# Query spread and page mask as fp32r products of split factors, the own token's value products moved behind the loop, penalties in one VectorE operation

## What is computed

```python
gate = jnp.einsum('bshd,bnhd->bhsn', q, k_mean)         # 8 blocks of 256 past tokens
_, idx = lax.top_k(gate, ks)                            # keep 3 blocks per head
s_sel = jnp.where(ok_sel, s_sel - slopes * dist_sel, NEG)
p = jax.nn.softmax(concatenate([s_sel, s_own]), axis=-1)
o = einsum('bhqnj,bhqnjd->bqhd', p_sel, v_sel) + einsum('bhqj,bjhd->bqhd', p_own, v_own)
```

## Time and profile before

| what | value |
| --- | --- |
| median of the runs | 651.88 us (650.3 to 652.17) |
| the profiled execution | 652.33 us |
| its span, first to last instruction | 650.6 us |
| mean granted TensorE clock | 0.921 |
| TensorE busy | 580.1 us (89% of the span), 4100 products |
| VectorE busy | 406.6 us (62%), 608 instructions |
| ScalarE busy | 272.9 us (42%) |
| GpSimd busy | 133.9 us (21%) |

### The profile page before, as it was taken

How to read it: one execution, slowest core, us unless ns; L and a number is a source line. 1 busy time by engine, 2 the same in 40 slices (tenths; PEclk the granted TensorE clock), 3 DMA queues, 4 the chain that set the end, 5 groups by cost and what they waited for, 6 DMA issues and landing times.

```text
span 650.6 us, 10200 instructions
## 1 busy us (share of the span) xinstructions
PE 580.1 (89%) x4100; PEld 468.8 (72%) x4100; DVE 406.6 (62%) x608; ACT 272.9 (42%) x492; POOL 133.9 (21%) x205
## 2 busy tenths in 40 slices
PE   3869998899999899999988688779999999999997
PEld 2647776664554647566547587668999999999997
DVE  2423794589888799888664284446645566655541
ACT  1102213195857668563463152127333343433341
POOL 8110020075757476570000000000000000000000
PEclk9969999878979799797978798987999999999999
DMA  7997289437999989979850949625487746366600
GB/s 254 380 405 301 93 335 400 147 116 296 361 368 325 383 304 409 347 286 374 300 236 9 379 149 369 217 91 203 143 279 243 253 138 210 91 178 179 178 34 33
DMA packets 85198, 159.29 MB, mean 245 GB/s; under 512 B 2572, under 2 KB 61112, under 8 KB 81047
## 3 DMA queue, kind: packets, MB, share of 16 engines
q1 hardware_dynamic: 79328, 89.27, 41.3%
q0 software_dynamic: 5120, 67.71, 26.3%
q10 hardware_dynamic: 703, 1.67, 0.7%
HBM read 156.39 MB, written 2.72 MB: 245 GB/s over the span
## 4 chain that ended last, share of the span: by engine, by line
PE 68%; DVE 14%; DMA 8%; ACT 6%; issue 3%; ACTq 1%; SPq 1%; POOL 1%; DVEq 0%; POOLq 0%
PE acc L1211 15%; PE acc L1306 12%; PE acc L1307 12%; PE acc L1308 11%; PE chain L1330 5%; PE acc L1178 3%; DVE sall L862 2%; DVE prod L855 2%; DMA wring<-in_w_ada 2%; DMA wring<-in_w_out 2%; PE small L1368 2%; ACT L515 2%; DMA wring<-in_w_attn_proj 1%; DMA wring<-in_w_ffn_in 1%; PE chain L1332 1%
## 5 line engine op out<-in xcount | busy, mean ns | idle before, releaser
L1211 PE MATMUL acc<-hT,wring 128*128 128x264 f32 x576 | 160.4, 433 | 4.0 <-DVE hT L820 1.9
L933 DVE TENSOR_TENSOR wlo<-wring,whi 128x1024 fp32r<-128x1024 f32 (+2 forms) x92 | 101.9, 1108 | 99.0 <-ACT whi L515 98.3
L1211 PEld LDWEIGHTS acc<-hT,wring 128*128 128x128 f32 x576 | 118.6, 214 | 35.5 <-issue 10.8
L515 ACT ACTIVATE whi<-wring 128x1024 fp32r<-128x1024 f32 (+2 forms) x92 | 88.0, 963 | 118.6 <-PE acc L1308 94.0
L1306 PE MATMUL acc<-xlo,whi 128*128 128x264 f32 x416 | 123.9, 298 | 13.1 <-DVE xT L1081 7.0
L1307 PE MATMUL acc<-xhi,wlo 128*128 128x264 f32 x416 | 121.0, 291 | 0.0
L1308 PE MATMUL acc<-xhi,whi 128*128 128x264 f32 x416 | 120.9, 291 | 0.0
L487 POOL TENSOR_TENSOR cvT<-cvT,cprod 128x256 f32<-128x256 f32 x120 | 87.2, 727 | 81.7 <-ACT cprod L515 66.2
L1306 PEld LDWEIGHTS acc<-xlo,whi 128*128 128x128 f32 x416 | 81.3, 195 | 17.8 <-DVE wlo L933 8.2
L1307 PEld LDWEIGHTS acc<-xhi,wlo 128*128 128x128 f32 x416 | 81.7, 196 | 0.1
L1308 PEld LDWEIGHTS acc<-xhi,whi 128*128 128x128 f32 x416 | 81.2, 195 | 0.0
(11 more groups left out here) (222 smaller groups left out, 647.5 us busy)
## 6 DMA issues: line engine op xcount, KB each, us to landing
wring<-in_w_ada SPq DMA_DIRECT2D x24, 1024.0 KB, 8.1
wring<-in_w_ffn_in SPq DMA_DIRECT2D x22, 1024.0 KB, 6.6
wring<-in_w_in SPq DMA_DIRECT2D x12, 1024.0 KB, 18.1
wring<-in_w_ffn_out SPq DMA_DIRECT2D x16, 704.0 KB, 5.7
wring<-in_w_out SPq DMA_DIRECT2D x4, 1024.0 KB, 14.9
wring<-in_w_in SPq DMA_DIRECT2D x6, 512.0 KB, 9.6
wring<-in_w_in SPq DMA_DIRECT2D x4, 768.0 KB, 8.4
wring<-in_w_conv_proj SPq DMA_DIRECT2D x2, 1024.0 KB, 9.6
```

The source lines that it names most:

```text
L515: return nc.scalar.activation(out, in_, f, **kw)
L933: v.tensor_tensor(wlo[:, place, 0:n, :], w, whi[:, place, 0:n, :].bitcast(F32), ALU.subtract)\
L1211: ins = mm(bank[:, 0:R], w[:, k, P * t:P * t + P], src[:, k, :], start=k == 0, stop=k == KD - 1)
```

## The change

1. The bank `qs` gets the samples' queries twice, in rows 0 to 7 and 32 to 39. ScalarE copies both to `qsplit`, rounded to fp32r, and a third time to `snat`; VectorE subtracts the rounded rows from the bank in rows 32 to 39. `spread_query` is one fp32r product over 40 rows with `qsel`.
2. The distance penalty becomes a product of two rows (`posal`, fp32r) in place of the identity times a table; `inquad` and `pen` are fp32r too.
3. L988 and L990 become one operation with a table `bars` (the diagonal times NEG), made at the start.
4. The own token's probabilities are put aside for each sample (`powns`, in place of L1038); its product in `weigh_values` is gone. Behind the loop VectorE picks the diagonal, multiplies the own values (`vrow`), TensorE turns them (four products), and VectorE adds them to `oT`.
5. `snat`, `vrow`, `ptable` lie in other tensors; GpSimd makes the new tables at the start.

```diff
@@ -565,7 +584,10 @@
             bank = when_full(act, "qs")
-            freed(func(snat[:, :], bank[0:B, :], ACT.Copy), "qs")
+            act.wait_ge(consts, 3)
+            func(qsplit[32:32 + B, :], bank[32:32 + B, :], ACT.Copy).then_inc(qs_ready, 1)
+            func(qsplit[0:B, :], bank[0:B, :], ACT.Copy).then_inc(qs_ready, 1)
+            func(snat, bank[0:B, :], ACT.Copy).then_inc(qs_ready, 1)
...
+            bank = when_full(dve, "qs")
+            dve.wait_ge(qs_ready, 3)
+            freed(v.tensor_tensor(qsplit[32:32 + B, :], bank[32:32 + B, :], qsplit[32:32 + B, :].bitcast(F32),
+                                  ALU.subtract), "qs")
...
-                mm(qbc[b % 2][:, :], ident[0:B, b:b + 1].to_broadcast([B, P]), snat[:, :], start=True, stop=True)\
+                mm(qbc[b % 2][:, :], qsel[0:32 + B, b:b + 1].to_broadcast([32 + B, P]), qsplit[0:32 + B, :],
+                   start=True, stop=True)\
                     .then_inc(qbc_ready, 1)
...
-            to_rows("qs", qT, S, B)
+            bank = bank_for("qs")
+            for t in range(4):
+                nc.tensor.transpose(bank[0:B, P * t:P * t + P], qT[:, t, S:R], ident[:, :])
+                ins = mm(bank[32:32 + B, P * t:P * t + P], qT[:, t, S:R], ident[:, :], start=True, stop=True)
+            ins.then_inc(acc_full, 1)
@@ -985,10 +1012,8 @@
-                at_pen = mark(v.tensor_scalar(gate[:, :], gate[:, :], float(TOPK), NEG, ALU.is_ge, ALU.mult))
-                dve.wait_ge(dve_step, at_pen)
-                v.tensor_tensor(pen[:, :, :], gate[:, :].unsqueeze(2).to_broadcast([H, NB, H]),
-                                ident[0:H, 0:H].unsqueeze(1).to_broadcast([H, NB, H]), ALU.mult)\
+                v.scalar_tensor_tensor(pen[:, :, :], gate[:, :].unsqueeze(2).to_broadcast([H, NB, H]), float(TOPK),
+                                       bars[:, :].unsqueeze(1).to_broadcast([H, NB, H]), ALU.is_ge, ALU.mult)\
                     .then_inc(pen_ready, 1)
...
-                v.scalar_tensor_tensor(pown, s1[32:32 + B, PG, :], ident[32:32 + B, 32 + b:33 + b], rinv[32:32 + B, :],
-                                       ALU.mult, ALU.mult).then_inc(p_ready, 1)
+                v.tensor_tensor(powns[32:32 + B, b, :], s1[32:32 + B, PG, :], rinv[32:32 + B, :], ALU.mult)\
+                    .then_inc(own_ready, 1)
@@ -1322,14 +1363,12 @@
-                        ins = mm(pv[32 * q:32 * q + H, :], pg[:, g, :], vring[:, g, :], start=g < 4, stop=PG - 4 < g)
-                        if g == PG - 4:
-                            mm(pv[0:H, :], pown, vrow, start=False, stop=True)
+                        ins = mm(pv[32 * q:32 * q + H, :], pg[:, g, :], vring[:, g, :], start=g < 4, stop=PG - 4 <= g)
...
-                mm(mask_, ident[:, :], alib[:, :, :].rearrange("p g h -> p (g h)"), start=True, stop=False)
+                mm(mask_, posal[:, 0, :], posal[:, 1, :], start=True, stop=False)
                 for e in range(QU):
-                    ins = mm(mask_.rearrange("p (c j h) -> p c j h", c=CH, h=H), inquad[:, e, :],
+                    ins = mm(mask_.rearrange("p (c j h) -> p c j h", c=CH, h=H), inquad[0:H, e, :],
@@ -1049,7 +1074,18 @@
             for t in range(1, KD):
                 conv_branch(t)
+                if t == 1:
+                    dve.wait_ge(own_ready, B)
+                    step(v.tensor_tensor(powns[32:32 + B, :, :], powns[32:32 + B, :, :],
+                                         ident[32:32 + B, 32:32 + B].unsqueeze(2).to_broadcast([B, B, H]), ALU.mult))
+                    step(v.tensor_reduce(pown, powns[32:32 + B, :, :].rearrange("p b h -> p h b"), AX.X, ALU.add))
+                    v.tensor_tensor(vrow.rearrange("p (h d) -> p h d", d=DH), vrow.rearrange("p (h d) -> p h d", d=DH),
+                                    pown.unsqueeze(2).to_broadcast([B, H, DH]), ALU.mult).then_inc(ownrow_ready, 1)
                 if t == 2:
+                    dve.wait_ge(ownt_ready, 1)
+                    dve.wait_ge(o_ready, 2 * B)
+                    v.tensor_tensor(oT[:, :, S:R], oT[:, :, S:R], ownT.rearrange("p (t b) -> p t b", b=B), ALU.add)\
+                        .then_inc(ownt_ready, 1)
                     for k in range(AT):
...
-                    act.wait_ge(o_ready, 2 * B)
+                    act.wait_ge(ownt_ready, 2)
...
             turn_values(B - 1)
+            pe.wait_ge(ownrow_ready, 1)
+            for t in range(AT):
+                ins = mm(ownT[:, B * t:B * t + B], vrow[:, P * t:P * t + P], ident[32:32 + B, 32:32 + B], start=True, stop=True)
+            ins.then_inc(ownt_ready, 1)
             for t in range(2, KD):
```

More of the change, by code:

```diff
@@ L145, in program @@
         prT = sb("prT", [P, 384])
-        srows = sb("srows", [P, A])
-        snat, vrow = srows[0:B, :], srows[32:32 + B, :]
+        qsplit = sb("qsplit", [P, A], F32R)
+        qsel = sb("qsel", [P, B], F32R)
         ident = sb("ident", [P, P])
@@ L177, in program @@
         cmp1, cmp2 = (mrow[0:H, 0, 64 * e:64 * e + 64].rearrange("p (m n) -> p m n", m=NB) for e in range(2))
-        pen = sb("pen", [H, NB, H])
+        pen = sb("pen", [H, NB, H], F32R)
+        spots = pvm[:, P:2 * P]
+        powns = gs[:, :, 0:H]
         tiny = sb("tiny", [P, 64])
@@ L181, in program @@
                                        tiny[:, 32:40], tiny[32:32 + B, 40:48])
+        bars = tiny[0:H, 56:64]
         pmx, psum_, prin = tiny[:, 48:50], tiny[:, 50:52], tiny[:, 52:54]
         cvs = sb("cvs", [P, CT, B])
-        ptable = sb("ptable", [P, B * PG], I32)
+        ptable = pr[:, 256:384].bitcast(I32)
         lane = sb("lane", [P, 1])
@@ L241, in program @@
         spread_max, spread_sum = small[:, 0:H], small[:, 16:16 + H]
-        pv, pvT = chain, psT[:, 384:392]
+        pv, pvT, ownT = chain, psT[:, 384:392], small[:, 256:256 + AT * B]
         vec_in, x_in, c_in, st_in, pt_in = sem("vec_in"), sem("x_in"), sem("c_in"), sem("st_in"), sem("pt_in")
@@ L442, in _ @@
                 step(g.memset(slopes[:, h:h + 1], -2.0 ** (-8.0 * (h + 1) / H)))
-            step(g.iota(dists[:, :].rearrange("p (c j) -> p c j", c=CH), pattern=[[-PC * P, CH], [-1, PC]], base=PAST,
-                        channel_multiplier=-PC, allow_small_or_imprecise_dtypes=True))
-            step(g.tensor_tensor(alib[:, :, :], dists[:, :].unsqueeze(2).to_broadcast([P, PG, H]),
-                                 slopes[:, :].unsqueeze(1).to_broadcast([P, PG, H]), ALU.mult))
+            two = slice(0, 2)
+            step(g.iota(dists[two, :].rearrange("p (c j) -> p c j", c=CH), pattern=[[-PC * P, CH], [-1, PC]], base=PAST,
+                        channel_multiplier=0, allow_small_or_imprecise_dtypes=True))
+            step(g.affine_select(out=dists[two, :], in_=dists[two, :], compare_op=ALU.not_equal, fill=-float(PC),
+                                 base=-1, pattern=[[0, PG]], channel_multiplier=1))
+            step(g.iota(spots[two, :], pattern=[[1, P]], base=0, channel_multiplier=0,
+                        allow_small_or_imprecise_dtypes=True))
+            step(g.affine_select(out=spots[two, :], in_=spots[two, :], compare_op=ALU.not_equal, fill=1.0,
+                                 base=0, pattern=[[0, P]], channel_multiplier=1))
             step(g.memset(lower[:, :, :], 1.0))
@@ L449, in _ @@
                                  base=0, pattern=[[1, NB], [-1, NB]], channel_multiplier=0))
-            step(g.memset(inquad[:, :, :], 0.0))
+            step(g.memset(inquad[:, :, :].bitcast(F32), 0.0))
             for q in range(QU):
-                step(g.memset(inquad[:, q, 32 * q:32 * q + 32], 1.0))
+                step(g.memset(inquad[0:H, q, 32 * q:32 * q + 32].bitcast(F32), 1.0))
+            step(g.tensor_copy(posal[:, 0, :], spots[two, :]))
+            step(g.tensor_tensor(posal[:, 1, :].rearrange("p (g h) -> p g h", h=H),
+                                 dists[two, :].unsqueeze(2).to_broadcast([2, PG, H]),
+                                 slopes[two, :].unsqueeze(1).to_broadcast([2, PG, H]), ALU.mult))
+            step(g.memset(qsel[:, :].bitcast(F32), 0.0))
+            step(g.tensor_copy(qsel[0:B, :], ident[0:B, 0:B]))
+            step(g.tensor_copy(qsel[32:32 + B, :], ident[32:32 + B, 32:32 + B]))
+            step(g.memset(qsplit[:, :].bitcast(F32), 0.0))
             step(g.memset(headof[:, :], 0.0))
```

14 lines of the change are left out of this document (9 added, 5 removed).

## The result

| | before | changed |
| --- | --- | --- |
| median (range, runs) | 652.02 us (650.3 to 654.83, 4) | **634.68 us** (634.5 to 636.54, 4) |
| ratio, 95% interval | | **0.9736** [0.9698, 0.9775] |
| profiled execution | 652.33 us | 634.61 us |
| span, mean granted clock | 650.6 us, 0.921 | 632.9 us, 0.933 |

The change is faster by 17.3 us. The forecast was 7.6 us, and its range ended at 640. The order of the work came out as predicted, but the loop gained nearly twice as much.

The account below looks back on a forecast made before the run. The chain of waits was 68% TensorE, 14% VectorE. Gains of 10.4 us in the loop and penalties of 2.8 at start and end made -7.6: 644.7 us profiled, median 644.3; forecast 641.5 to 647, full range 640.0 to 651.5.

Parts of the forecast that it names:

- Ranking beside GpSimd: VectorE's block ranking, b=1 to 5, still ends with GpSimd's gather issue; only L990 goes, 1.0 us gained.
- GpSimd doesn't hold the ranking: Rival: the earlier arrival finds other gaps between GpSimd's additions; up to 3.7 us more gain, 640.6 us; chance 0.10.
- The mask: TensorE, mask to tile: five fp32r instructions replace ten; 1.0 to 1.1 us saved a cycle, 6.2 over six cycles.
- Narrow fp32r is no cheaper: Rival: each of the mask's five products costs as much as its pair; 2.0 us saved, not 6.2; 648.5 us; chance 0.27.
- The third part: TensorE's stretch of the cycle through mask, half a tile and turned maximum; from tile to next first sum forecast 0.
- The clock rival: Rival: TensorE idle or on tiny products before the mask lengthens lower-clock stretches; 12.9 us lost, 657.2 us; chance 0.09.
- The end: Behind the loop, last weighing to attention load: wait for the own row queues units 2 to 7; +2.1 us, bounds 0 to +4.
- The start: Before the loop: spread query adds matmuls, copies and a subtraction, first multiplication 1.4 later, 0.7 regained; +0.7 us.
- VectorE's idle time before the gate's copy gone: Sign that the forecast is right: VectorE, idle 0.74 us before the gate's copy, has no idle time there in b=1 to 5.
- L977's successor still at 0.60 beside additions: Sign that the forecast is right: this VectorE ranking operation still takes 0.5 us or more beside GpSimd's additions.
- b=6: Cycle where GpSimd adds nothing: VectorE's idle 0.74 and L990's 0.2 count in full; 0.95 us gained.
- cycle b=0: Loop's cycle where ScalarE is behind with four stores and the tap products: mask gain forecast as nothing.

Follow-up runs that it names:

- The fillers: The changed kernel plus three unread f32 products of 264 columns where TensorE waits for the penalty, each cycle: 629.05 us, ratio 0.9684.

## Why the prediction was wrong

**The failed step is "Ranking beside GpSimd".** It took one phase of the two engines for a rule: L977 ended 0.07 behind the additions and L988 with the issue, so the ranking would end with GpSimd's work whatever came earlier. What the rows fit is a smaller thing. A VectorE operation that reads two tensors in SBUF (L977) ends when the addition that is under way ends, not the last one. The additions follow one another every 0.85 (5.10/6). In the changed kernel the fifth ends at about 176.98 + 5 x 0.853 = 181.25, and L1004 is done there, at 181.27. The penalty's operation L1015 is held in its turn, by the sixth (0.39 us, where it has 0.21 in b=0 and 6). In the kernel before L977 happened to meet the sixth and last. In all cycles b=1 to 5 of both kernels the operation ends 0.07 to 0.08 us behind an addition. So an earlier gate moves the whole ranking, and the 0.95 that I kept as an upper bound was not even the end: 1.2 in each of five cycles, 5.3 us more than forecast. In b=2 the gate's copy comes 0.82 us earlier behind the first sum (5.95 to 5.13), and from there the ranking is 0.4 shorter: 0.24 for the operation that is gone, 0.08 each in L1001 and L1010. The rival "GpSimd doesn't hold the ranking" had 0.10; it was right that the earlier arrival counts, and its price (0.95 a cycle, 3.7 us more in all) was too low.

The statement of the Trainium skill (GPSIMD Engine Reference, Specifications) that GpSimd contends with VectorE is borne out by L977, 0.61 beside additions and 0.20 without. How long the ranking is held I drew from one phase of the rows myself, and the forecast without it, 3.7 us lower, would have been the better one.

**The mask was right in kind.** Five narrow fp32r products take 0.70 at the full clock, 0.14 each, and 1.25 at the lower, 0.25 each; the forecast had 0.12 and 0.24. Where it fell short by 0.8 is that two or three of the six masks now run at the full clock. The rival "Narrow fp32r is no cheaper" is false.

**The third part was costed at nothing** and gave 2.2 us. Low stretches are 6.7 us shorter (37.4 to 30.7). The fillers show the direction: with no low stretch at all the third parts of b=1 to 6 add up to 100.1 us in place of 104.8. The clock rival had the wrong sign. It counted TensorE's longer wait before the mask, which is there (1.50 for 0.82). Why the stretches became shorter all the same is open: the own product's move alone left them at 37.6, the mask alone brought 34.1. Its rule from TensorE: Matmul & The Clock Gate in the Trainium skill (Why this matters for your kernels), that gaps bring the lower clock, agrees with the trace in that fillers in the gap keep the full clock (0.90 to 1.00 over the loop); but the gap grew from 0.82 to 1.50 and the stretches did not, so the gap alone did not decide here.

**The end** cost 3.2 for 2.1. The wait for the own row was named and is 4.37. Mis-sized were two things. The turning of the own row took 1.87 in place of 0.95, at the lower clock, which makes the way from unit 0 to unit 2 10.1 us where I had 9.2 (6.2 before). And unit 0 started 4.1 behind the last weighing's start, 1.3 earlier for 1.8, as the value gather was late. Unit 2 ran at the lower clock before the change as well (0.42 us a product in both), and from its start to the load 0.6 were added for the 0.9 forecast. I had named no transfer there: a loop 16 us shorter brings the last gather onto the path.

**The start** cost nothing that shows, where I had +0.7. The steps up to the first multiplication are 2.2 longer, but the execution's first 60 us were 2.7 shorter, which differs by as much between other runs (the first sum of b=0 lies between 120.3 and 125.2 in the kernels above). The load of the attention's weights took 6.90 in place of 8.47, and all that follows it is the same to 0.1 us; nothing here explains the shorter load. From its start to the end the kernels above differ as much, 292.8 to 296.8 us.

Right were: VectorE's idle time before the gate's copy gone, L977's successor still at 0.60 beside additions, b=6, cycle b=0, and the order of waits behind the loop.

## What to carry to other kernels

Where two engines contend, read which instruction is held and until which event, and check in a second cycle with another phase; one phase that repeats is no rule, since the change itself shifts it. When a loop gets shorter, look again at every transfer that was early and at the engine that was second. Where TensorE must wait behind short products, take side work out from ahead of the wait, then try products that nobody reads in it, and look in the trace whether they begin before the clock falls; put the side work where its consumer isn't queued yet. Beside every profile, look how typical its execution is of the kernel's others, by time and by mean clock.

## What was unexpected about the hardware

- GpSimd's issue of a gather held a VectorE TENSOR_SCALAR of 8x8 (0.41 us in place of 0.16) but not a SCALAR_TENSOR_TENSOR of 8x64 with two inputs (0.21 inside the issue). GpSimd's additions held both: the TENSOR_SCALAR took 0.33 and ended 0.02 us behind an addition, L977 took 0.61 for 0.20, L1015 0.39 for 0.21. An operation that began 0.03 ahead of an addition (L1010, 0.21 us) was not held.
- Products without a reader made the kernel 5.6 us faster (634.68 to 629.05, ratio 0.9684 with an interval that overlaps the change's own), and with the own product's move alone 13 us (648.12 to 635.17, the intervals apart, mean clock 0.913 to 0.920 without them and 0.949 to 0.959 with them).
- A product on one quarter of the bank in the middle of sixteen on four quarters cost 1.9 us in the cycle (5.5 to 3.6), and where it stood, fillers behind it did not keep the clock up in the profiled executions. Whether its form does that or the 2 us by which it delays the fillers was not tried.
